# Turning the hidden activations of two MLPs in VectorE blocks and SBUF-to-SBUF transfers instead of TensorE transposes

## The reference, cut to what matters

```python
D_MODEL = 2048; SEQ = 256; D_FF = 4 * D_MODEL
# first block
h2 = rmsnorm(x, norm2_g[l])
x = x + jnp.square(jax.nn.relu(h2 @ w_mlp_in[l])) @ w_mlp_out[l]
# second block
h2 = rmsnorm_2(x, g_mlp[l])
x = x + jnp.square(jax.nn.relu(h2 @ w_up[l])) @ w_down[l]
```

## Time and profile before

| | |
|---|---|
| median of 3 runs | 2931.09 us (2930.93 to 2931.25) |
| the profiled execution's own time | 2930.9 us |
| its span in the profile | 2928.9 us |
| TensorE matmul busy | 2901.3 us (99% of the span), 13892 instructions |
| TensorE weight load busy | 2397.7 us (82%) |
| VectorE busy | 1725.1 us (59%) |
| ScalarE busy | 1367.5 us (47%) |
| DMA engines | q1 holds them 60.0% of the span, 559 MB |
| first MLP, second MLP | about 842 to 1564 us and 2204 to 2920 us of the span |

### The profile page before, as it was taken

The page is one execution under the profiler, slowest core; times in us unless marked ns, Lnnn a source line. Parts: engine busy times, 40 slices in busy tenths (PEclk is TensorE's granted clock), DMA queues, the critical chain, the costliest instruction groups (busy, mean ns, idle before and its releaser), DMA issues.

```text
span 2928.9 us, 33931 instructions
## 1 busy us (share of the span) xinstructions
PE 2901.3 (99%) x13892; PEld 2397.7 (82%) x13892; DVE 1725.1 (59%) x1858; ACT 1367.5 (47%) x1570; POOL 2.5 (0%) x7
## 2 busy tenths in 40 slices
PE   8999999999999999999999999999999999999998
PEld 7888878888888888888888888888888888888886
DVE  6688844466654455554556678765655555455555
ACT  6644434554454444444445444444454444444443
POOL 0000000000000000000000000000000000000000
PEclk9999999999999999999999999999999999999999
DMA  9566755556655556555657666666556565656554
GB/s 310 156 200 197 204 166 188 170 166 187 210 183 188 192 186 197 189 182 187 196 183 229 189 179 197 194 201 205 182 185 205 180 195 182 198 180 201 187 180 158
DMA packets 290746, 561.14 MB, mean 192 GB/s; under 512 B 17696, under 2 KB 24480, under 8 KB 289952
## 3 DMA queue, kind: packets, MB, share of 16 engines
q1 hardware_dynamic: 290592, 558.98, 60.0%
HBM read 556.81 MB, written 2.10 MB: 191 GB/s over the span
## 4 chain that ended last, share of the span: by engine, by line
PE 96%; DVE 2%; ACT 1%; issue 1%; DMA 0%; SPq 0%; DVEq 0%; ACTq 0%
PE ACC L581 92%; PE TB L537 2%; DVE WL L1242 1%; DMA RAW<-in_w_in_dram 0%; ACT WH L832 0%; PE TB L619 0%; DVE CA L1734 0%; ACT JK L850 0%; DVE X L1676 0%; DVE WGC L1782 0%; PE TB L652 0%; PE TB L655 0%; DVE X L1634 0%; PE TB L661 0%; PE TB L673 0%
## 5 line engine op out<-in xcount | busy, mean ns | idle before, releaser
L1242 DVE TENSOR_TENSOR WL<-RAW,WH 128x1024 fp32r<-128x1024 f32 (+1 forms) x1024 | 1232.9, 1219 | 860.3 <-ACT WH L832 857.8
L832 ACT ACTIVATE WH<-RAW 128x1024 fp32r<-128x1024 f32 (+1 forms) x1024 | 1062.9, 1053 | 934.4 <-PE ACC L581 898.5
L581 PE MATMUL ACC<-WH,XTH 128*128 128x512 f32 (+1 forms) x1696 | 666.4, 393 | 14.1 <-DVE WL L1242 13.3
L581 PE MATMUL ACC<-WH,XTL 128*128 128x512 f32 (+1 forms) x1696 | 658.0, 388 | 0.0
L581 PE MATMUL ACC<-WL,XTH 128*128 128x512 f32 (+1 forms) x1696 | 657.6, 388 | 0.0
L581 PE MATMUL ACC<-WH,XBH 128*128 128x512 f32 x1024 | 402.3, 393 | 1.5 <-DVE WL L1242 1.5
L581 PE MATMUL ACC<-WH,XBL 128*128 128x512 f32 x1024 | 399.1, 390 | 0.0
L581 PE MATMUL ACC<-WL,XBH 128*128 128x512 f32 x1024 | 398.6, 389 | 0.0
L581 PEld LDWEIGHTS ACC<-WH,XTH 128*128 128x128 f32 x1696 | 319.0, 188 | 82.4 <-issue 11.3
L581 PEld LDWEIGHTS ACC<-WH,XTL 128*128 128x128 f32 x1696 | 318.8, 188 | 66.1
L581 PEld LDWEIGHTS ACC<-WL,XTH 128*128 128x128 f32 x1696 | 319.2, 188 | 62.9
(11 more groups left out here) (252 smaller groups left out, 1606.7 us busy)
## 6 DMA issues: line engine op xcount, KB each, us to landing
RAW<-in_w_in_dram SPq DMA_DIRECT2D x256, 512.0 KB, 4.3
RAW<-in_w_mlp_in_dram SPq DMA_DIRECT2D x128, 512.0 KB, 4.2
RAW<-in_w_mlp_out_dram SPq DMA_DIRECT2D x128, 512.0 KB, 4.6
RAW<-in_w_up_dram SPq DMA_DIRECT2D x128, 512.0 KB, 4.0
RAW<-in_w_down_dram SPq DMA_DIRECT2D x128, 512.0 KB, 4.5
RAW<-in_w_gate_dram SPq DMA_DIRECT2D x96, 512.0 KB, 4.3
RAW<-in_w_branch_dram SPq DMA_DIRECT2D x48, 512.0 KB, 4.5
RAW<-in_w_out_dram SPq DMA_DIRECT2D x32, 512.0 KB, 4.5
```

Source lines behind the costliest of these rows:

```text
L581: ins = e.matmul(ACC[:, 2 * (b % 2) + half, 0:n], p[:, k, xs], q[:, t, 0:n], start=(k == 0 and m == 0), stop=(k == nk - 1 and m == 2))
L832: e.activation(WH[u % NSPL][:, :, 0:n], RAW[u % NRAW][:, :, 0:n], ACT.Copy).then_inc(hi, 1)
L1242: e.tensor_tensor(l, r, h, ALU.subtract).then_inc(lo, 1)
```

## The change

The TensorE transposes of the hidden blocks, their 8 uses of PSUM banks per group and the two-step copies out of them go. In their place, for each hidden block:

1. One unit behind *last*, VectorE (`hidden_turn`) transposes `HB` within 32x32 blocks into a new tile `HT`, one instruction of 128x512 per token half. It waits for the square, and for the transfers of the hidden block before, since `HT` has one buffer. After it, a token block t (32 tokens) lies on partitions 32t to 32t+31, but these now hold 32 columns each of all four partition groups g.
2. In SyncE's order at units *last*+9 to *last*+12, ahead of each of these units' weight load, four transfers each (16 in all) move `HT`'s partitions 32t to 32t+31 to partitions 32g to 32g+31 of a new tile `YT`: 32 partitions x 2 halves x 128 elements, 32 KB, in contiguous pieces of 512 bytes. The first waits for `hidden_turned` and until VectorE has split the hidden block before (`hid_lo`), since `YT` has one buffer.
3. Eleven units behind *last*, ScalarE (`hidden_split`) copies `YT` to `YAH` or `YBH` in one instruction of 1024 elements per partition, whose pattern puts the tokens in order, and VectorE subtracts in one instruction.

The matmuls of o(j,0) wait for `hid_lo` in place of the PSUM banks. `HT` and `YT` take 8 KB more per partition in each MLP.

```diff
@@ 
+    hid_turned, hid_hi, hid_lo = sem("hidden_turned"), sem("hidden_hi"), sem("hidden_lo")
+    ld_hid = sem("ld_hidden")
...
+    HT["1"], YT["1"] = sb("HT1", [P, 2, 4, P], F32, m1), sb("YT1", [P, 8, P], F32, m1)
...
+    HT["2"], YT["2"] = sb("HT2", [P, 2, 4, P], F32, m2), sb("YT2", [P, 8, P], F32, m2)
...
+    HN = {(tag, j, b): 16 * n + 2 * j + b for n, tag in enumerate("12") for j in range(8) for b in range(2)}
@@ the order
                 at(("ev", "h" + tag), last("h" + tag, j, b))
-                at(("hid", tag, j, b), last("h" + tag, j, b) + 2, 2)
+                at(("hid_turn", tag), last("h" + tag, j, b) + 1)
+                at(("hid_split", tag), last("h" + tag, j, b) + 11)
@@
+    def by_tokens(y):
+
+        return y.rearrange("p k (t i) -> p t k i", t=8)
@@ SyncE, ahead of the weight load of unit u
+            for tag, j, q in HN:
+                t = u - last("h" + tag, j, q) - 9
+                if 0 <= t < 4:
+
+                    hn = HN[tag, j, q]
+                    if t == 0:
+                        e.wait_ge(hid_turned, hn + 1)
+                        if hn > 0:
+                            e.wait_ge(hid_lo, hn)
+                    for g in range(4):
+                        e.dma_start(YT[tag][32 * g:32 * g + 32, :, :].rearrange("p (h t) n -> p h t n", h=2)[:, :, t, :],
+                                    HT[tag][32 * t:32 * t + 32, :, g, :]).then_inc(ld_hid, 16)
@@ TensorE
-                if name[2] == 0:
-                    emptied(e, ("hid" + tag, j, i // 2), i % 2)
+                if name[2] == 0 and i % 2 == 0:
+                    e.wait_ge(hid_lo, HN[tag, j, i // 2] + 1)
...
-        def hidden(tag, j, b):
-            for k in range(2):
-                if k == 0:
-                    e.wait_ge(hid, (0 if tag == "1" else 16) + 2 * j + b + 1)
-                t, done = bank(("hid" + tag, j, b), k)
-                transposes(t, lambda m, half: HB[tag][b][:, half, (2 * k + m) * P:(2 * k + m) * P + P]).then_inc(done, 1)
-                yield
@@ ScalarE
                     if j > 0:
-                        filled(e, ("hid" + tag, j - 1, b), 1)
+                        e.wait_ge(hid_turned, HN[tag, j - 1, b] + 1)
...
-            for k in range(2):
-                t = filled(e, use, k)
-                e.activation(yh[:, 4 * b + 2 * k:4 * b + 2 * k + 2, :], pair(t), ACT.Copy).then_inc(turned, 1)
-                yield
+                    e.wait_ge(ld_hid, 256 * (hn + 1))
+                    e.activation(by_tokens(yh[:, 4 * b:4 * b + 4, :]), YT[tag].rearrange("p t (k i) -> p t k i", k=4),
+                                 ACT.Copy).then_inc(hid_hi, 1)
+                    yield
@@ VectorE
-            for k in range(2):
-                s = slice(4 * b + 2 * k, 4 * b + 2 * k + 2)
-                low_part(yl[:, s, :], yh[:, s, :], copied, n0 + k + 1, use, k)
-                yield
+                    e.wait_ge(hid, hn + 1)
+                    if hn > 0:
+                        e.wait_ge(ld_hid, 256 * hn)
+                    for half in range(2):
+                        ins = e.transpose(HT[tag][:, half, :, :].rearrange("p g (k i) -> p k g i", k=4),
+                                          HB[tag][b][:, half, :].rearrange("p (k g i) -> p k g i", k=4, g=4))
+                    ins.then_inc(hid_turned, 1)
+                    yield
...
+                    e.wait_ge(hid_hi, hn + 1)
+                    e.tensor_tensor(by_tokens(yl[:, s, :]), YT[tag].rearrange("p t (k i) -> p t k i", k=4), by_tokens(yh[:, s, :]),
+                                    ALU.subtract).then_inc(hid_lo, 1)
```

More of the change, by code:

```diff
@@ L308, in build @@
         banks(task, 8, (0, 1, 2, 3))
-    for j in range(8):
-        for b in range(2):
-            banks(("hid1", j, b), 2, (2 * b, 2 * b + 1))
     banks("x2", 8, (0, 1, 2, 3))
@@ L319, in build @@
         banks(task, 8, (0, 1, 2, 3))
-    for j in range(8):
-        for b in range(2):
-            banks(("hid2", j, b), 2, (2 * b, 2 * b + 1))
     YA0 = {"gm0": 0, "gm1": 2, ("at_o", 0): 4, ("at_o", 1): 6}
[L326 to L330, removed]
+    HN = {(tag, j, b): 16 * n + 2 * j + b for n, tag in enumerate("12") for j in range(8) for b in range(2)}
     TX0 = {"m1": 0, "x1": 8, "x2": 16, "m2": 24, "x3": 32}
@@ L814, in _ @@
             tasks["turn", task] = lambda task=task, src=src: turn(task, src)
[L815 to L818, removed]
         run(e, stream, tasks)
@@ L1076, in hidden_out, with hidden_split @@
                     yield
[L1078 to L1084, removed]
-            for k in range(2):
-                t = filled(e, use, k)
-                e.activation(yh[:, 4 * b + 2 * k:4 * b + 2 * k + 2, :], pair(t), ACT.Copy).then_inc(turned, 1)
-                yield
+        def hidden_split(tag):
+            for j in range(8):
+                for b in range(2):
+                    hn, yh = HN[tag, j, b], YB[tag][0] if j % 2 else YAH
+                    if j >= 2:
+                        multiplied(e, "o" + tag, j - 2, 3)
+                    elif j == 0:
+                        multiplied(e, *{"1": ("bb", 3), "2": ("b2a", 3)}[tag])
+                    e.wait_ge(ld_hid, 256 * (hn + 1))
+                    e.activation(by_tokens(yh[:, 4 * b:4 * b + 4, :]), YT[tag].rearrange("p t (k i) -> p t k i", k=4),
+                                 ACT.Copy).then_inc(hid_hi, 1)
+                    yield
         def o_squares(tag, r):
@@ L1221, in _ @@
         for tag in ("1", "2"):
-            for j in range(8):
-                for b in range(2):
-                    tasks["hid", tag, j, b] = lambda tag=tag, j=j, b=b: hidden(tag, j, b)
+            tasks["hid_split", tag] = lambda tag=tag: hidden_split(tag)
         run(e, stream, tasks)
@@ L1660, in o_out, with hidden_turn, hidden_split @@
                     yield
-        def hidden(tag, j, b):
-            use = ("hid" + tag, j, b)
-            (yh, yl), copied, n0 = (YB[tag], yb_hi, YB0[use]) if j % 2 else ((YAH, YAL), ya_hi, YA0[use])
-            for k in range(2):
-                s = slice(4 * b + 2 * k, 4 * b + 2 * k + 2)
-                low_part(yl[:, s, :], yh[:, s, :], copied, n0 + k + 1, use, k)
-                yield
+        def hidden_turn(tag):
+            for j in range(8):
+                for b in range(2):
+                    hn = HN[tag, j, b]
+                    e.wait_ge(hid, hn + 1)
[6 more added lines that the diff above has]
+                    yield
+        def hidden_split(tag):
+            for j in range(8):
+                for b in range(2):
+                    hn = HN[tag, j, b]
+                    yh, yl = YB[tag] if j % 2 else (YAH, YAL)
+                    s = slice(4 * b, 4 * b + 4)
+                    e.wait_ge(hid_hi, hn + 1)
+                    e.tensor_tensor(by_tokens(yl[:, s, :]), YT[tag].rearrange("p t (k i) -> p t k i", k=4), by_tokens(yh[:, s, :]),
+                                    ALU.subtract).then_inc(hid_lo, 1)
+                    yield
         def block1_end():
@@ L1823, in _ @@
         for tag in ("1", "2"):
-            for j in range(8):
-                for b in range(2):
-                    tasks["hid", tag, j, b] = lambda tag=tag, j=j, b=b: hidden(tag, j, b)
+            tasks["hid_split", tag] = lambda tag=tag: hidden_split(tag)
+            tasks["hid_turn", tag] = lambda tag=tag: hidden_turn(tag)
         run(e, stream, tasks)
```

2 lines of the change are left out of this document (1 added, 1 removed).

## The result

| | before | after |
|---|---|---|
| median | 2931.17 us (2930.93 to 2931.33) | 2900.45 us (2900.1 to 2900.76) |
| profiled execution's own time | 2930.9 us | 2900.7 us |
| its span | 2928.9 us | 2898.3 us |

The ratio is 0.9895 [0.9878, 0.9912]. The change saves 30.7 us.

The account below looks back on a forecast made before the run. TensorE, busy 99% of the span at full clock, was taken to bound the kernel; -30.7 us for its transposes plus 0 for all added work gave 2900.2 profiled, 2900.4 us median, range 2893 to 2925.

Parts of the forecast that it names:

- TensorE's saving: In the MLPs, 64 groups of four transposes go, each priced 0.48 us from unit start times: 30.7 us saved.
- Room behind *last: On VectorE, cuts of *last*+3 and *last*+4 keep 0.7 and 0.8 us before TensorE wants them, so cost 0.
- the formula for its cost: VectorE ahead of the cut of *last*+4: 2T - 2.2 us per block for a transpose of T us over 1.1.
- Rival 2: VectorE's transpose is slow, delaying the cut of *last*+4: 2908 us at T = 1.22, 2980 at 2.35; chance 0.08.
- The queue: DMA engines: a transfer takes at most 0.16 us; weights 1.6 plus transfers 0.7 per unit, under 2.72; cost 0.
- Rival 1: Small transfers clog the DMA queue, delaying weight loads of *last*+9 to *last*+12: slower, 3039 us; chance 0.10.
- SyncE: At units with transfers, five issues of 0.51 us take 2.56 against 2.72 of pace: just fits, cost 0.
- Two of the prediction's signs of being right: In the MLPs: transfers issued at 0.5 us, and ScalarE's cuts waiting on TensorE and hardly on a load.
- Its sign of being wrong: ScalarE's cut waiting for MLP weights and TensorE for `WL` in units *last*+9 to *last*+12 of second blocks.
- Rival 3: SyncE issues slower than thought: at 0.8 us each, 1.1 us for each of 16 pairs, 17 us, 2918; chance 0.12.
- Its own sum for the third load: Lateness at SyncE with 0.8 us issues: 1.3 + 14 x 0.8 - 5.4 = 7.1, plus 0.6 for the queue, against 6.6.
- The cover: Weight loads of *last*+9 to *last*+12, late by 3.4, 3.2, 3.1, 2.9 us, have 6.6 us of room, the fourth 8.1; cost 0.

Follow-up runs that it names:

- Runs 1: Changed kernel with the 64 groups of four TensorE transposes put back, into PSUM banks nobody reads: 2930.68 us.
- run 2: Changed kernel without the 512 transfers, splits reading HT directly, five units sooner: 2899.85 us.
- run 6: Changed kernel with VectorE transposing every block twice, the first time into a tile nobody reads: 2916.24 us.
- runs 3: Changed kernel with the same transfers issued by GpSimd, 16 in a row once a block is turned: 2900.05 us, 2899.62 in a second run.
- run 7: Changed kernel with transfers in pieces of 128 bytes instead of 512, 256 a transfer, same bytes: 2902.08 us.
- run 5: Changed kernel with a block's 16 transfers ahead of two weight loads, eight each, instead of four ahead of each of four: 2997.88 us.
- run 4: Changed kernel with a block's 16 transfers all ahead of one weight load instead of four ahead of each of four: 3040.6 us.

## Why the prediction was right, point by point

- **TensorE's saving.** 64 x 0.48 = 30.7 us was forecast. Runs 1 and 2 have it as 31, again 0.48 a group. That the medians are 30.7 apart to the digit is in part luck: the MLPs gave back 29.9, since SyncE's issues cost them 1.1, and 0.7 came from the stretch between them. The price read from starts held, the busy time of 38.2 would have been a quarter too much.
- **VectorE.** 0.69 taken, 0.687 measured, 0.65 in a pair. Room behind *last* forecast as 0.7 and 0.8, found 0.6 and 1.0; the formula for its cost held in run 6. Rival 2 falls. The estimate of 1.24 us, worked out from the 311 ns that the Trainium skill's page "VectorE: DVE Perf Modes" (The three transpose paths) has for a bf16 tile of 128x128, isn't borne out: 0.687 decides.
- **ScalarE.** The reordering copy was charged nothing beyond its size: 1.043 against 1.06 by the cut's row.
- **The queue.** q1 holds the engines for 0.631 x 2898.3 - 0.600 x 2928.9 = 71.5 us more, 0.14 us per transfer; against run 2 (60.3% of 2897.5) it is 81.6 us, 0.16. At most 0.16 was forecast. Rival 1 falls, by runs 3 and 7 as well. Its argument against it had ten transfers in flight in the first 6 us; the trace has at most eight. By the rule in the Trainium skill's page "DMA: Bandwidth & Descriptors" (Bandwidth), that transfers under 64 KB are dominated by their descriptors, the estimate was 0.8 us. The page's figures are for loads from HBM issued by GpSimd; for these transfers from SBUF to SBUF, issued by SyncE, this trace doesn't agree: 0.14 to 0.16.
- **SyncE: the step that failed, without harm.** "So a unit with transfers needs 5 x 0.51 = 2.56 us of SyncE against 2.72 of pace: it just fits." It needs 3.18 and doesn't fit. The 0.51 came from large loads into an idle queue; an issue of this transfer takes 0.59 to 0.60, and 0.64 from one to the next. Two of the prediction's signs of being right failed with it: issues at 0.5 us, and ScalarE's cuts hardly waiting on a load (331 us). Its sign of being wrong, TensorE waiting for `WL` at *last*+12 of a second block, came once. Rival 3 had this mechanism, at 0.8 us. Its own sum for the third load gives 1.3 + 14 x 0.64 - 5.4 = 4.9 us at the measured 0.64, and the load is 5.0 late; by the same sum, with its 0.6 for the queue, a stall would begin at about 0.72. So the forecast held with less to spare than it says. The row of 1.29 us that it read as an issue "at full DMA engines" wasn't: their busy share there is 0.49.
- **The cover: right in its size, and used up faster than forecast.** Its parts can be read from the starts and ends of loads, cuts and matmuls in the changed kernel. Medians of the 16 second blocks, in us, with the forecast in brackets where it has one:

| load of unit | goes out behind the cut of u-4 | TensorE wants u behind that cut | cut of u ends behind the load | left |
|---|---|---|---|---|
| *last*+9 | 3.8 (3.4) | 13.5 (13.5) | 6.4 (6.9) | 3.3 |
| *last*+10 | 4.7 (3.2) | 13.9 | 6.6 | 2.7 |
| *last*+11 | 5.0 (3.1) | 13.8 | 6.8 | 1.9 |
| *last*+12 | 7.1 (2.9) | 15.4 (15.0) | 7.0 | 1.1 (5.2) |

  The interval and the 6.6 us of room held. The 4.6 us of landing that went into them is a median, not an upper end (3.9 to 5.9 in these places), but the sum of landing and cuts was right. What failed is the lateness, which was to shrink from load to load and grows. Of the 4.2 us that the last load is later than forecast, 1.9 are the pace of the issues, three units at 3.18 instead of 2.56, and 0.4 were there at the first load. The other 1.9 are the cuts: the forecast counts the lateness as if each followed 2.72 us behind the last, but they follow faster, and it counts that only as extra room (its 1.5 us), not as lateness. At *last*+12 the room left was 0.15 to 1.8 us in 15 of the 16 blocks and missing in one, the stall of 0.66. Eight issues ahead of a load (run 5) use up more than there is. Rival 3, which priced each us over that edge at one us per pair of blocks, was too mild: first blocks stall as well (runs 4 and 5), and TensorE can come back at half pace.

## What to carry to other kernels

Where one engine is busy 99% of the span, price work taken off it from the starts of its instructions with and without, and price work added elsewhere by the room of the next due piece at that place. Count every issuing instruction on the queue that feeds the bound engine: a few more per unit can be free and twice as many ahead of a load cost three times the gain (run 5), so spread them, or give them to an idle issuer and leave more time for landing. Behind a stall of some us the engine may come back at half pace. And before a median's half us is put down to anything, look at the same stretch in both traces.

## What the runs showed of the hardware that was not expected

- TensorE ran at half pace behind 18 of 32 idle times of 1.25 to 4.69 us: granted clock 0.57 over 3.3 us, then 1.00 (run 4). The 18 were of 2.52 to 4.69 us, the 14 without it of 1.25 to 3.22; what tells them apart between 2.52 and 3.22 is open.
- How long an issue takes SyncE depends on what it issued right before: a weight load 0.37 us by itself, 0.47 behind another load, 0.59 behind a transfer; a transfer 0.59 to 0.60, with 0.64 from one to the next. 20 of 1024 took 0.8 to 2.7 us; what holds those up is open.
- GpSimd's issues are as quick as SyncE's (0.53 us), their landing is 2.1 us later (4.7 against 2.6).
- 40960 more packets (512 bytes, and those that end a transfer) took 71.5 us of 16 engines, 28 ns of one engine each, or 32 against run 2; 98304 further ones, at 128 bytes and the same bytes in all, 9 ns each (run 7).
- A VectorE transpose whose output goes out in pieces of 32 elements takes no longer than a subtraction of its size (0.687 against 0.692 us).
